# Last mixer of a 567-chunk transformer kernel: the low weight parts of its xBC and z stages made by VectorE, the first short tap by ScalarE

## What is computed

```python
proj = h @ w_in                                   # glu_a 512, glu_b 512, z 1024, xbc 2048, dt 32 columns
g = glu_a * jax.nn.sigmoid(glu_b)
g = depthwise_conv(g, dw_w, dw_b, ...)            # 31 taps over 512 channels
g = jax.nn.silu(layer_norm(g, ln_g, ln_b))
xbc = jax.nn.silu(depthwise_conv(xbc, conv_w, conv_b, ...))   # 4 taps over 2048 channels
...                                               # state space scan of 16 heads in 4 groups over x, B, C = xbc
y = rms_norm(y * jax.nn.silu(z), norm_w)
return jnp.concatenate([g, y], axis=-1) @ w_out
```

## Time and profile before

| | us |
|---|---|
| median of 3 runs | 4063.26 (4062.07 to 4065.25) |
| the profiled execution | 4067.98 |
| its span on the core | 4066.2 |
| xbc and z stages, first eviction to last eviction (DVE) | 3239.34 to 3451.38 = 212.04 |

### The profile page before, as it was taken

How to read it: one execution, slowest core, us unless ns; L and a number is a source line. 1 busy time by engine, 2 the same in 40 slices (tenths; PEclk the granted TensorE clock), 3 DMA queues, 4 the chain that set the end, 5 groups by cost and what they waited for, 6 DMA issues and landing times.

```text
span 4066.2 us, 52151 instructions
## 1 busy us (share of the span) xinstructions
PE 3758.4 (92%) x19667; PEld 3124.5 (77%) x19667; DVE 1823.3 (45%) x2051; ACT 1221.3 (30%) x1849; POOL 1490.7 (37%) x619
## 2 busy tenths in 40 slices
PE   8888899999998999989998989998999877889998
PEld 8776799999975788868886768886888655567886
DVE  2552235446354554442336542335234599634224
ACT  3532232223134222232223432223222322533222
POOL 3221134444320344434444044444444423034444
PEclk9998899999997899999999999999999988999999
DMA  3110022222210122212222012222222211022222
GB/s 145 59 63 31 32 73 83 89 89 93 75 51 1 62 94 98 93 68 97 94 98 78 27 68 95 96 97 74 94 97 98 73 52 62 1 83 72 94 93 83
DMA packets 85400, 307.72 MB, mean 76 GB/s; under 512 B 9456, under 2 KB 9712, under 8 KB 85104
## 3 DMA queue, kind: packets, MB, share of 16 engines
q1 hardware_dynamic: 84816, 304.28, 21.5%
q10 hardware_dynamic: 416, 1.05, 0.1%
HBM read 303.19 MB, written 2.10 MB: 75 GB/s over the span
## 4 chain that ended last, share of the span: by engine, by line
issue 43%; PE 39%; POOL 15%; DVE 2%; POOLq 0%; DVEq 0%; ACT 0%; ACTq 0%
PE psum L308 36%; POOL w_lo L279 13%; POOL resid L703 2%; DVE square_sum L486 1%; PE psum L1652 1%; PE psum L1616 0%; DVE arena L926 0%; PE psum L523 0%; PE psum L1636 0%; PE psum L516 0%; DVE y_lo L914 0%; POOLq L278 0%; DVE arena L924 0%; DVEq L925 0%; POOLq L235 0%
## 5 line engine op out<-in xcount | busy, mean ns | idle before, releaser
L279 POOL TENSOR_TENSOR w_lo<-w_raw,w_hi 128x1024 fp32r<-128x1024 f32 x567 | 1421.8, 2508 | 2516.6 <-ACT w_hi L272 2516.6
L272 ACT ACTIVATE w_hi<-w_raw 128x1024 fp32r<-128x1024 f32 x567 | 600.4, 1059 | 2106.4 <-PE psum L308 2082.7
L308 PE MATMUL psum<-x_hi,w_hi 128*128 128x512 f32 (+1 forms) x2936 | 991.8, 364 | 75.2 <-POOL w_lo L279 73.7
L308 PE MATMUL psum<-x_lo,w_hi 128*128 128x512 f32 (+1 forms) x2936 | 987.6, 363 | 0.0
L308 PE MATMUL psum<-x_hi,w_lo 128*128 128x512 f32 (+1 forms) x2936 | 982.7, 361 | 0.0
L308 PE MATMUL psum<-y_hi,w_hi 128*128 128x264 f32 (+1 forms) x2528 | 735.3, 336 | 41.1 <-DVE arena L1064 18.8
L308 PE MATMUL psum<-y_lo,w_hi 128*128 128x264 f32 (+1 forms) x2528 | 736.1, 337 | 0.0
L308 PE MATMUL psum<-y_hi,w_lo 128*128 128x264 f32 (+1 forms) x2528 | 733.2, 336 | 0.0
L308 PEld LDWEIGHTS psum<-x_hi,w_hi 128*128 128x128 f32 x2936 | 528.7, 190 | 182.1 <-POOL w_lo L279 88.0
L308 PEld LDWEIGHTS psum<-x_lo,w_hi 128*128 128x128 f32 x2936 | 526.4, 190 | 88.3 <-issue 1.4
L308 PEld LDWEIGHTS psum<-x_hi,w_lo 128*128 128x128 f32 x2936 | 527.3, 191 | 86.5
(11 more groups left out here) (384 smaller groups left out, 3091.7 us busy)
## 6 DMA issues: line engine op xcount, KB each, us to landing
w_raw<-in_weights SPq DMA_DIRECT2D x567, 512.0 KB, 3.2
resid<-in_xT SPq DMA_DIRECT2D x8, 264.0 KB, 7.5
out_dram<-resid SPq DMA_DIRECT2D x8, 256.0 KB, 2.0
arena<-in_lru_w SPq DMA_DIRECT2D x1, 1024.0 KB, 9.9
rope_sb<-in_rope SPq DMA_DIRECT2D x1, 528.0 KB, 11.4
mats<-in_mats SPq DMA_DIRECT2D x1, 512.0 KB, 10.1
rope_sb<-in_rope ACTq DMA_DIRECT2D x1, 512.0 KB, 3.7
arena<-in_pool_inv ACTq DMA_DIRECT2D x1, 512.0 KB, 4.4
```

The lines of the kernel that those rows point to most:

```text
L272: nc.scalar.activation(WH[:, (n + c) % 2, :], RAW[:, (n + c) % 4, :], ACT.Copy).then_inc(high_ready, 1)
L279: nc.gpsimd.tensor_tensor(WL[:, (n + c) % 2, :], RAW[:, (n + c) % 4, :], WH[:, (n + c) % 2, :], ALU.subtract).then_inc(low_ready, 1)
L308: last = mm(o[:, a, :], wt[:, ws, k * P:k * P + P], x[:, k, a * (w // banks):(a + 1) * (w // banks)], start=(k == 0 and p == 0), stop=(k = ...
```

## The change

For the 24 chunks 461 to 484 (xbc's third up to o_out_g's second, `BY_DVE`) DVE makes the low part (`low_weights`) and counts it on a semaphore of its own, `low_by_dve`. POOL skips these chunks. Every wait for a low part (PE's and SP's) goes through `low_wait`, which chooses the semaphore and the count; SP's loop of loads is cut into three. In the xbc steps the order on DVE is now eviction, gated taps, low part, then the short taps; the first short tap is made by ACT (Identity with scale and bias), which signals `o_ft`, and ACT's Silu of step c-1 stands behind the first tap of step c.

```diff
+        BY_DVE = CHUNKS["xbc"] + 2, CHUNKS["o_out_g"] + 2
+        def low_wait(eng, n, i=0, c=0):
+            at = n + c + 1
+            if BY_DVE[0] <= n + c < BY_DVE[1]:
+                eng.wait_ge(low_by_dve, 4 * i + at - BY_DVE[0])
+            elif n + c >= BY_DVE[1]:
+                eng.wait_ge(low_ready, 4 * i + at - (BY_DVE[1] - BY_DVE[0]))
+            else:
+                eng.wait_ge(low_ready, 4 * i + at)
...
             def step(i, c, waits=False):
-                pe.wait_ge(low_ready, 4 * i + n + c + 1)
+                low_wait(pe, n, i, c)
...
             act.wait_ge(st["o_gp"], 1)
+            def activated(c):
+                act.wait_ge(st["o_cv"], c + 1)
+                nc.scalar.activation(XBC[:, c, 0:T2], CV[:, c % 2, 0:T2], ACT.Silu).then_inc(st["o_si"], 1)
             for c in range(16):
                 split_high(act, CHUNKS["xbc"] + 2, 0, c)
...
-                act.wait_ge(st["o_cv"], c + 1)
-                nc.scalar.activation(XBC[:, c, 0:T2], CV[:, c % 2, 0:T2], ACT.Silu).then_inc(st["o_si"], 1)
+                act.wait_ge(st["o_si"], max(c, 1))
+                act.wait_ge(psum_free, CHUNKS["xbc"] + c + 1 + 4)
+                nc.scalar.activation(CV[:, c % 2, 0:T2], STG[:, c % 2, 0:T2], ACT.Identity, bias=vec("sconv_b", c),
+                                     scale=vec("sconv_w", c)).then_inc(st["o_ft"], 1)
+                if c:
+                    activated(c - 1)
+            activated(15)
...
+            def low_weights(n):
+                dve.wait_ge(high_ready, n + 1)
+                tt(WL[:, n % 2, :], RAW[:, n % 4, :], WH[:, n % 2, :], ALU.subtract).then_inc(low_by_dve, 1)
...
                 tt(x[:, 2:2 + T2], acc(CHUNKS["xbc"], c)[:, 0, :], RS[:, 0:T2], ALU.mult).then_inc(psum_free, 1)
-                dve.drain()
-                dve.wait_ge(st["o_si"], c + 1)
-                last = ts(o, x[:, 0:T2], vec("sconv_w", c), vec("sconv_b", c), ALU.mult, ALU.add)
+                if c == 0:
+                    dve.wait_ge(st["o_si"], 1)
+                taps(c)
+                low_weights(CHUNKS["xbc"] + c + 2)
+                dve.wait_ge(st["o_ft"], c + 1)
                 for j in range(1, 4):
                     dve.drain()
                     last = stt(o, x[:, j:j + T2], vec("sconv_w", 16 * j + c), o, ALU.mult, ALU.add)
                 last.then_inc(st["o_cv"], 1)
-                taps(c)
...
                 tt(SZ[c], acc(CHUNKS["z"], c)[:, 0, :], RS[:, 0:T2], ALU.mult).then_inc(psum_free, 1)
+                low_weights(CHUNKS["z"] + c + 2)
                 taps(16 + c)
...
+                if name == "oddp":
+                    pool_stream(pool, at, CHUNKS["xbc"] + 2)
+                    at = CHUNKS["o_out_g"] + 2
                 pool_stream(pool, at, end)
```

More of the change, by code:

```diff
@@ L176, in build @@
         raw_loaded = [sem(f"raw_loaded{i}") for i in range(4)]
-        high_ready, low_ready = sem("high_ready"), sem("low_ready")
+        high_ready, low_ready, low_by_dve = sem("high_ready"), sem("low_ready"), sem("low_by_dve")
         tile_done, psum_free = sem("tile_done"), sem("psum_free")
@@ L198, in build @@
             "e_pt", "e_ptc", "e_ptd", "e_pv", "e_o", "e_ot", "inv_loaded",
-            "o_dt", "o_ab", "o_tr", "o_cv", "o_si", "o_xt", "o_xc", "o_cb", "o_cc", "o_xs", "o_of", "o_oe", "o_bc",
+            "o_dt", "o_ab", "o_tr", "o_ft", "o_cv", "o_si", "o_xt", "o_xc", "o_cb", "o_cc", "o_xs", "o_of", "o_oe", "o_bc",
             "o_gp", "o_w", "o_m", "o_y", "o_yd", "o_z", "o_g", "o_gc", "o_mu", "o_xm", "o_sl")}
@@ L252, in load_chunk, with loads @@
             sp.dma_start(RAW[:, slot, :], weights[n]).then_inc(raw_loaded[slot], 16)
-        def stream(sp):
[L255 to L264, removed]
+        BY_DVE = CHUNKS["xbc"] + 2, CHUNKS["o_out_g"] + 2
[7 more added lines that the diff above has]
+                eng.wait_ge(low_ready, 4 * i + at)
+        def stream(sp):
+            def loads(begin, end):
+                first, last = -(-begin // 4), end // 4
+                for n in range(begin, 4 * first):
+                    low_wait(sp, n - 4)
+                    load_chunk(sp, n, n % 4)
+                with sp.Fori(0, last - first) as i:
+                    for c in range(4):
+                        low_wait(sp, 4 * first + c - 4, i, 0)
+                        load_chunk(sp, 4 * i + 4 * first + c, c)
+                for n in range(4 * last, end):
+                    low_wait(sp, n - 4)
+                    load_chunk(sp, n, n % 4)
+            loads(4, BY_DVE[0] + 4)
+            loads(BY_DVE[0] + 4, BY_DVE[1] + 4)
+            loads(BY_DVE[1] + 4, N_CHUNKS)
         def split_high(act, n, i, c):
@@ L552, in first_tiles @@
             pe.wait_ge(psum_free, n + 4)
-            pe.wait_ge(low_ready, n + 2)
+            low_wait(pe, n + 1)
             w = width(n)
```

## The result

The changed kernel takes 4034.62 us (median of 4 runs, 4029.7 to 4038.91). The kernel before takes 4064.26 us beside it (4 runs, 4062.07 to 4068.96). The ratio is 0.9923, with a 95% interval of 0.9908 to 0.9938. On another chip, with six runs of the change, it came to 4029.57 us against 4063.98, ratio 0.992 (0.9905 to 0.9935).

What follows compares the result with a forecast made beforehand. DVE was taken to bound the xbc and z stages. The terms -50.1 - 9.9 + 26.2 + 0.75 = -33.0 us, set off from the median 4063.3, gave 4030.3 us, range 4023 to 4042.

Steps and rivals of the forecast that it cites:

- POOL silent: Xbc and z stages: without POOL's low parts, DVE's taps lose no time beside them; 1.79 + 23 x 2.10 = 50.1 us less.
- First short tap off DVE: Xbc steps: ACT makes this tap, saving DVE 0.62 us in each of 16 steps, 9.9 us less; gaps stay as many.
- Low part on DVE: Xbc and z steps: 1.14 us each, upper bound 1.49; 23 ahead of the last eviction, 26.2 us more.
- Silu of step 15: End of xbc: `rates(15)` waits for ACT's Silu, now uncovered by gated taps; 0.75 us more, once.
- The 24th low part: Z step 7: delays gated taps' end and `scaled_rows(0)` by 1.14 us, not the eviction; covered by 5 us, nothing.
- ACT's first tap: Xbc steps: ready 1.4 us after eviction began, wanted at 4.7, so nothing; if uncovered, up to 0.64 us a step.
- The wait for the high part: DVE's wait for `high_ready` ahead of its low part costs nothing; at worst 0.3 us in a z step.
- SP: SP's waits for low parts follow the same chunks, four ahead, with DMA at 55 GB/s in xbc: costs nothing.
- PE as what is late next: Xbc and z: PE becomes the bound in part, every second tile 1 us late, 12 us back, 4042 us; chance 0.09.
- The rival of a quicker scan: Before the scores: PE's idle 12.27 us becomes about 7, scan begins up to 3 us quicker, 4027 us; chance 0.08.
- The slower rival: Low part in fp32r on DVE takes 4.7 us instead of 1.14, 82 us more, 4112 us; chance 0.03.

## Why the prediction was right, point by point

The forecast was 4030.3 us, in a range of 4023 to 4042; the measured median is 4034.62, and 4029.57 on the other chip.

1. *POOL silent, -50.1.* Held. Taps of four take 2.74 us in every step; the group of all 116 in the stages is 747 ns each. That the cause is POOL's read is shown by the reads that were added and took it back, and by the memsets that didn't.
2. *First short tap off DVE, -9.9, with as many drains as before.* Held: the run with low parts alone is 9.2 us longer than the changed kernel, and 9.9 - 0.75 (item 4) = 9.15.
3. *Low part on DVE, 1.14 each, +26.2.* Held at its lower bound. The row of L2274 was the right one to go by; the two taps end to end (1.49) were not needed.
4. *Silu of step 15, +0.75.* Held: 0.77 us idle.
5. *The 24th low part is covered.* Held: nothing changed behind the last eviction, 614.8 us.
6. *ACT's first tap, covered.* The effect held, but its price was wrong. I took 0.64 us, the Silu's; ACT's rows in that step and the group of all 16:

```profile
3301.60 0.82 ACT L2106 ACTIVATE arena<-arena,vecs_sb 128x512 f32<-128x512 f32 x1 [3.43 <-DVE arena L2282]
3302.32 0.62 ACT L2086 ACTIVATE arena<-arena 128x512 f32<-128x512 f32 x1
...
L2106 ACT ACTIVATE arena<-arena,vecs_sb x16: 801/816/820, 3244.3 to 3362.0; 128x512 f32<-128x512 f32 x16
L2086 ACT ACT_TABLE_LOAD  x4: 1283/1283/1283, 3252.4 to 3341.1; - x4
```

   It begins when the eviction ends and is done at 3302.42, 1.6 us after the eviction began; DVE wants it at 3305.56. So 3.1 us of cover were left. The table loads are four as before, which is what the Trainium skill says ("ScalarE: Activation LUTs", "Table sets: the hidden batching unit": identity is in every set).
7. *The wait for the high part, nothing.* Held in the changed kernel: no row of DVE waits for it. It came up where I moved the low part to the front of the step, once, and in the run without gated taps, five times and 2.3 us in all.
8. *SP, nothing.* Held: no engine's wait in the stages ends with a load, and DMA moves 67 GB/s instead of 55 with the shorter steps.

**PE as what is late next.** It was not. PE still has a gap ahead of each tile, of some 1.4 us in xbc, and DVE ends it:

```profile
3358.66 0.50 PE L326 MATMUL psum<-x_hi,w_hi 128*128 128x512 f32 x1 [1.39 <-DVE w_lo L2274]
```

I had argued that shorter gaps would not lengthen the slow pieces. They grew fewer: the clock went from 0.87 to 0.93 and 0.99 in the two stages. It was worth nothing, because PE isn't the bound there. The run without gated taps shows where it would be: 5.56 us a step.

**The rival of a quicker scan** (4027) had the right sign for the gap but no gain:

```profile
3423.94 1.19 PE L1991 MATMUL psum<-arena 128*128 128x512 f32 x1 [6.14 <-ACT arena L2114]
```

PE's gap ahead of the scores shrank from 12.27 us to 6.14, as I had said (about 7), and the time behind the last eviction stayed 614.8. The traces show why: the scores begin 1.97 us after the last eviction before and 1.98 after the change, and in both the granted clock stands at 0.50 when they begin and for some 3 to 4 us more, so the eight of them take 5.73 us in both. The shorter gap did not spare the scan its slow start, and on that the rival had counted.

**The slower rival** rested on L914's 2.35 us as a price of the fp32r output. It fell: 1.22 us, shown twice.

**What lies between 4030.3 and 4034.62.** The stage gave 0.6 us more than forecast. The 4.3 us by which the first median came out above stand for nothing in the change; the first profile shows 4.15 us ahead of the stages, and the second, 8 us earlier than the kernel before, shows the opposite. The six runs on the other chip have their median 0.7 us from the forecast. The sum could be set off from the median, as I did, or from the profiled execution (4067.98 - 33.0 = 4034.9). The first median lies 0.3 us from the latter, the second 0.7 us from the former, and neither closeness is more than luck: the difference of the stages was forecast to 0.6 us, the level is not known to better than some 5 us. The two medians differ from the kernel before by 29.6 and 34.4 us, on either side of the stage's 33.6.

## What to carry to other kernels

If a VectorE instruction with two inputs in SBUF takes several times its shortest duration, look on GpSimd's timeline for an instruction that reads SBUF beside it: moving that work to VectorE can pay even when VectorE is the bound, here 1.14 us added for 2.1 us that were lost. Judge an edit by the stretch that it touches (178.47 and 178.46 us in two executions) and not by the total, which moved by 12 us for the same program. Whether a stage is bound by an engine is settled by adding to it and taking from it, and the second also shows how much room is left: here 1.7 us a step.

## What the runs showed of the hardware that I had not expected

- **What the lock costs goes with POOL's instruction and with what it meets.** A POOL low part of some 2.6 us cost 2.08 to 2.12 us in the gated taps, 1.93 in the short taps, where it began before the first of them (3306.97 against 3307.41); the subtraction, 1.90 us at its shortest, cost 1.47. Each of these is some 0.4 to 0.6 us less than POOL's duration. Where POOL's subtraction began just before a low part of DVE, its row was 3.27 us long and the loss of the step still 1.46 (8.71 us against 7.25).
- **Only some instructions hold, and only some are held.** The memset of POOL cost nothing 24 times. The Trainium skill ("SBUF — State Buffer", "Who interferes with whom") has both sides: two-input DVE instructions are held by GpSimd's reads, "not with one that only writes it"; the trace agrees, 178.70 against 213.73 us. The rows also show DVE instructions with one tensor input held: the first short tap, 0.55 us long, took 2.34 beside POOL, and a CAST of 32x512 took 1.58 instead of 0.42 in the run with POOL's reads. And a DVE instruction with two inputs of which one is in PSUM isn't held. In the kernel before, in an earlier stage, DVE and POOL ran side by side so:

```profile
1788.42 2.29 DVE L914 TENSOR_TENSOR y_lo<-arena,y_hi 128x512 f32 x1 [0.82 <-ACT y_hi L882]
1790.64 0.68 DVE L908 TENSOR_TENSOR arena<-psum,scale 128x512 f32<-128x512 f32 x1
...
1787.81 5.15 POOL L279 TENSOR_TENSOR w_lo<-w_raw,w_hi 128x1024 fp32r<-128x1024 f32 x2 [5.39 <-ACT w_hi L272]
```

  L914, two inputs from SBUF, takes 2.29 us; L908, one from PSUM, takes 0.68 inside POOL's second instruction.
- **The first tap takes longer on ACT than a Silu**: 0.82 us for Identity with a per-channel scale and bias against 0.62 to 0.64 for the Silu with neither, on the same 128x512. That scale and bias are the reason and not the function is likely, but no run here has one without the other.
- **A drain costs about 0.16 us on DVE.** Three short taps with a drain ahead of each start (2.40 - 0.75) / 2 = 0.83 us apart, four gated taps without (2.74 - 0.75) / 3 = 0.66. Two drains fewer in each step gave 0.36 us.
